# One encoder layer on one core: the rows of the input projection dealt to partitions in another order, each chunk loaded by eight DMAs

## The reference, cut to what matters

```
mod = silu(c) @ w_cond + b_cond                      # 6 x 1024: shift, scale, gate, twice
h   = LN(x) * (1 + scale_m) + shift_m
proj = h @ w_in                                      # w_in: 1024 x 8208
qa, ka, va, ga, lra, qb, kb, vb, gate_a, gate_b = split(proj)
log_a = log_sigmoid(lra @ w_gla_a2 + b_gla_a) / 16   # lra: columns 3072..3087 of w_in
mix = w_out( sig(gate_a) * w_branch_a(GLA) + sig(gate_b) * w_branch_b(StickBreak) )
x   = LN1(alpha * x + gate_m * mix)
x   = LN2(alpha * x + gate_f * HierMoE(h2))          # 32 experts, each 1024x512, 1024x512, 512x1024
```

## Time and profile before

| | |
|---|---|
| runs | 1111.52 us median of 3 (1110.47 to 1113.07) |
| the profiled execution | 1114.87 us, span 1113.1 us from first to last instruction |
| busy, share of the span | PE 83%, PEld 57%, DVE 32%, ACT 29%, POOL 31% |
| granted TensorE clock | mean 0.926 of full speed |
| `w_in` chunks | 16 DMAs of 2 MB, median 13.8 us from issue to landing |
| stages | head to about 43 us, `w_in` groups to about 428 us, branches and output to about 544 us, routing to about 600 us, experts to the end |

### The profile page before, as it was taken

How to read it: one execution, slowest core, us unless ns; L and a number is a source line. 1 busy time by engine, 2 the same in 40 slices (tenths; PEclk the granted TensorE clock), 3 DMA queues, 4 the chain that set the end, 5 groups by cost and what they waited for, 6 DMA issues and landing times.

```text
span 1113.1 us, 14515 instructions
## 1 busy us (share of the span) xinstructions
PE 927.2 (83%) x5835; PEld 639.0 (57%) x5843; DVE 355.6 (32%) x763; ACT 318.9 (29%) x496; POOL 343.7 (31%) x280
## 2 busy tenths in 40 slices
PE   3888999898998988998656999999988888888840
PEld 3677989895997987788643344343433333333310
DVE  4200155926322124453564222222211211122108
ACT  2372343351886587233131010000000000000001
POOL 7544467760342434457100111111111111111011
PEclk9898999998999999899856999999999999999985
DMA  9726525438476753257653999999999999999832
GB/s 332 231 76 115 111 78 111 96 98 235 144 156 231 170 209 115 85 178 290 248 223 113 395 424 425 426 425 426 424 425 426 425 428 426 424 426 426 364 144 61
DMA packets 60820, 294.10 MB, mean 264 GB/s; under 512 B 7541, under 2 KB 9165, under 8 KB 48162
## 3 DMA queue, kind: packets, MB, share of 16 engines
q1 hardware_dynamic: 49296, 272.68, 66.3%
q0 software_dynamic: 6560, 11.45, 3.0%
q10 hardware_dynamic: 4914, 9.28, 2.4%
HBM read 290.22 MB, written 14.68 MB: 274 GB/s over the span
## 4 chain that ended last, share of the span: by engine, by line
PE 49%; DMA 30%; DVE 9%; ACT 6%; issue 4%; SPq 1%; POOL 1%; ACTq 0%; POOLq 0%; DVEq 0%
DMA ring<-in_w_exp_up 20%; PE bank L1363 13%; PE bank L1028 7%; PE bank L1029 6%; PE bank L1030 6%; PE bank L1386 5%; DMA ring<-in_w_in 5%; DMA cond_slot<-in_w_cond 4%; PE bank L981 1%; PE bank L1353 1%; DVE hf L1878 1%; PE bank L1083 1%; DMA ring<-expert_rows 1%; PE bank L1375 1%; DVE stats L1440 1%
## 5 line engine op out<-in xcount | busy, mean ns | idle before, releaser
L517 POOL TENSOR_TENSOR w_lo<-ring,w_hi 128x1024 fp32r<-128x1024 f32 x88 | 210.7, 2407 | 214.8 <-ACT w_hi L727 214.5
L1363 PE MATMUL bank<-ring,hf 128*64 128x512 f32 x1024 | 232.5, 607 | 23.0 <-DMA ring<-in_w_exp_up 22.0
L1028 PE MATMUL bank<-h_hi,w_hi 128*128 128x320 f32 x576 | 188.3, 327 | 20.1 <-POOL w_lo L517 7.9
L1030 PE MATMUL bank<-h_hi,w_lo 128*128 128x320 f32 x576 | 182.5, 317 | 0.0
L1363 PEld LDWEIGHTS bank<-ring,hf 128*64 128x64 f32 x1024 | 82.0, 140 | 170.6 <-issue 169.4
L1386 PE MATMUL bank<-ring,he 128*64 128x512 f32 x512 | 127.5, 643 | 0.9 <-DVE he L1882 0.5
L1028 PEld LDWEIGHTS bank<-h_hi,w_hi 128*128 128x128 f32 x576 | 112.6, 195 | 25.6 <-ACT va L668 5.8
L1029 PE MATMUL bank<-h_lo,w_hi 128*128 128x320 f32 x384 | 122.1, 318 | 0.0
L566 POOL DMA_INDIRECT xrow<-expert_inputs,sidx x32 | 32.7, 1022 | 263.3 <-DVE sidx L1868 263.3
L1030 PEld LDWEIGHTS bank<-h_hi,w_lo 128*128 128x128 f32 x576 | 112.4, 195 | 0.0
L727 ACT ACTIVATE w_hi<-ring 128x1024 fp32r<-128x1024 f32 x88 | 92.6, 1054 | 46.5 <-DMA ring<-in_w_in 27.6
(11 more groups left out here) (366 smaller groups left out, 1264.3 us busy)
## 6 DMA issues: line engine op xcount, KB each, us to landing
ring<-in_w_exp_up SPq DMA_DIRECT2D x32, 2048.0 KB, 34.8
ring<-in_w_exp_down SPq DMA_DIRECT2D x32, 2048.0 KB, 34.1
ring<-in_w_exp_gate SPq DMA_DIRECT2D x32, 2048.0 KB, 30.2
ring<-in_w_in SPq DMA_DIRECT2D x16, 2048.0 KB, 13.8
cond_slot<-in_w_cond SPq DMA_DIRECT2D x9, 2048.0 KB, 11.0
ring<-in_w_cond SPq DMA_DIRECT2D x3, 2048.0 KB, 17.1
ring<-in_w_branch_b SPq DMA_DIRECT2D x2, 2048.0 KB, 7.8
ring<-in_w_branch_a SPq DMA_DIRECT2D x2, 2048.0 KB, 10.1
```

The lines of the kernel that those rows point to most:

```text
L517: pool.tensor_tensor(w_lo[slot][:, :, c], raw[:, :, c], w_hi[:, :, c].bitcast(F32), ALU.subtract)\
L1028: mm(b, hi[:, k, c], x_hi[:, k, :], start=(k == 0), stop=False)
L1030: last = mm(b, lo[:, k, c], x_hi[:, k, :], start=False, stop=(k == KT - 1))
L1363: last = mm(bank[1][64 * q:64 * q + 64, :], xg[:, k % 4, k // 4, :], ring[s + q][:, k * FF:k * FF + FF], start=(k == 0), stop=(k == KT - 1 ...
```

## The change

Within each k-tile the 128 features are dealt to the partitions in another order: with `128 k + 16 i + e` for a feature (`i` of 8, `e` of 16), it now lies on partition `8 e + i`. The chunks of `w_in` and the low-rank columns are loaded by eight DMAs each, one for every `i`: DMA `i` writes partitions `i`, `i + 8`, ..., `i + 120`, of each eight runs (one a k-tile), and reads sixteen neighbouring rows of every k-tile. The other matrices are loaded as before. To match, the normalised `x` is written in the dealt order (DVE), the shift and scale rows are copied into `crow` in the dealt order (ACT, chunks 0 to 3), and the sixteen bias rows of shift and scale are loaded once more, dealt by a DVE copy and turned by a TensorE transpose of their own, for which the first transpose's successor waits (`bias_ready`). The load of the low-rank columns moves from ACT's queue to SP's, behind the four `w_cond` chunks of the head and ahead of the first `w_in` chunk.

```diff
--- before.py
+++ after.py
@@ -54,6 +54,7 @@
 NORM_BANKS = ((3, 4), (1, 2), (3, 4))
 NORM_ORDER = (0, 1, 3, 2, 4, 5)
 COND_ORDER = (0, 2, 1, 3)
+IN_PARTS = 8
 
 
 EXTRA = ("cr", "ct", "vat", "vbt")
@@ -219,6 +220,8 @@
         lraT = ab[1][0:32, 0:T]
         wa2 = sp_[1][0:32, :]
         rows = ab[0][:, 0:P]
+        bias_rows = ab[0][0:16, P:2 * P]
+        bias_spread = ab[0][0:16, 2 * P:3 * P]
         xt = vb
         xn = on
         ck = wgt
@@ -304,7 +307,7 @@
         bank = [ctx.enter_context(nc.psum_tensor(f"bank{i}", [P, 512], F32)) for i in range(8)]
 
 
-        names = """const_ready rows_in x_in lra_in misc_in vecs_in x1_in cols_t silu_ready mod_ready xn_ready xn_t xt_ready
+        names = """const_ready rows_in bias_ready x_in lra_in misc_in vecs_in x1_in cols_t silu_ready mod_ready xn_ready xn_t xt_ready
             h_dve h_act h_pool hi_ready lo_ready lra_hi lra_lo h_moved ob_hi_ready ob_lo_ready cond_in
             proj_ready taken_act taken_dve xla_ps la_ready b_ps b_ready dec_ready exp_ready pd_ready lev_ps
             lev_taken lev_added kd_ready ke_ready ke_t ket_ready st_ps st_ready qe_ready go_ps go_ready ck_t
@@ -338,10 +341,18 @@
 
         USED = ("gu_ps", "gu_ps", "down_ps")
 
+        def loads(slot, upto):
+
+            return sum(IN_PARTS if c[0] == "in" else 1 for c in DENSE[:upto] if c[2] == slot)
+
+        def spread(block):
+
+            return block.rearrange("r (e i) -> r i e", i=IN_PARTS)
+
         def arrived(i):
 
             slot = DENSE[i][2]
-            return (S["cond_in"] if slot == COND_SLOT else chunk_in[slot]), 16 * sum(c[2] == slot for c in DENSE[:i + 1])
+            return (S["cond_in"] if slot == COND_SLOT else chunk_in[slot]), 16 * loads(slot, i + 1)
 
         def base(e):
 
@@ -349,7 +360,7 @@
 
         def expert_use(s, turn):
 
-            before = sum(c[2] == s for c in DENSE) if s <= HI_SLOT else 0
+            before = loads(s, ND) if s <= HI_SLOT else 0
             return 16 * (before + turn + 1)
 
         USES = [len(range(b, E, 3)) for b in range(3)]
@@ -376,7 +387,14 @@
             sp.dma_start(rows[0:8, :], a["c_prompt"].rearrange("a (k p) -> (a k) p", p=P)).then_inc(S["rows_in"], 16)
             sp.dma_start(rows[8:16, :], a["c_sample"].rearrange("a (k p) -> (a k) p", p=P)).then_inc(S["rows_in"], 16)
             sp.dma_start(rows[16:64, :], a["b_cond"].rearrange("a (k p) -> (a k) p", p=P)).then_inc(S["rows_in"], 16)
+            sp.dma_start(bias_rows, a["b_cond"].rearrange("a (k p) -> (a k) p", p=P)[0:16, :]).then_inc(S["rows_in"], 16)
             sp.dma_start(rows[64:72, :], a["gla_norm_g"].rearrange("a h (j p) -> (a h j) p", p=P)).then_inc(S["rows_in"], 16)
+
+            def rows_apart(dst, c0, c1, signal):
+
+                src = SRC["in"].rearrange("(k i e) n -> i e k n", k=KT, i=IN_PARTS)
+                for i in range(IN_PARTS):
+                    sp.dma_start(dst[i::IN_PARTS], src[i][:, :, c0:c1]).then_inc(signal, 16)
 
             def freed(i):
 
@@ -387,6 +405,8 @@
 
             for i in sorted(range(ND), key=freed):
                 name, c0, slot = DENSE[i]
+                if i == 4:
+                    rows_apart(w_lra[:, :, :], 3072, 3088, S["lra_in"])
                 before = [n for n in range(i) if DENSE[n][2] == slot]
                 if before:
                     sp.wait_ge(*consumed(before[-1]))
@@ -394,8 +414,11 @@
                     sp.wait_ge(S["go_ps"], 6)
                     sp.wait_ge(S["st_ready"], 4)
                 src = SRC[name].rearrange("(k p) n -> p k n", p=P)[:, :, c0:c0 + CB]
-                dst = cond_slot if slot == COND_SLOT else ring[slot]
-                sp.dma_start(dst[:, :].rearrange("p (k n) -> p k n", k=KT), src).then_inc(arrived(i)[0], 16)
+                dst = (cond_slot if slot == COND_SLOT else ring[slot])[:, :].rearrange("p (k n) -> p k n", k=KT)
+                if name == "in":
+                    rows_apart(dst, c0, c0 + CB, arrived(i)[0])
+                else:
+                    sp.dma_start(dst, src).then_inc(arrived(i)[0], 16)
 
 
             sp.wait_ge(S["proj_ready"], group_index("bb", KT - 1) + 1)
@@ -631,7 +654,6 @@
             act.dma_start(xt[:, 0:2, :], a["x_prompt"][0].rearrange("(t p) d -> p t d", p=P)).then_inc(S["x_in"], 16)
             act.dma_start(xt[0:64, 2, :], a["x_sample"][0]).then_inc(S["x_in"], 16)
             act.wait_ge(S["const_ready"], 1)
-            act.dma_start(w_lra[:, :, :], a["w_in"][0].rearrange("(k p) n -> p k n", p=P)[:, :, 3072:3088]).then_inc(S["lra_in"], 16)
             act.dma_start(wa2[0:RANK, :], a["w_gla_a2"][0]).then_inc(S["lra_in"], 16)
             act.dma_start(wa2[RANK:RANK + 1, :], a["b_gla_a"]).then_inc(S["lra_in"], 16)
             act.wait_ge(S["cols_t"], 1)
@@ -646,7 +668,10 @@
                 src = bank[n % PROJ_BANKS]
                 act.wait_ge(S["proj_ready"], n + 1)
                 if name == "cr":
-                    ins = X.activation(crow[:, :], src[:, 0:P], ACT.Copy)
+                    if i < 4:
+                        ins = X.activation(spread(crow[:, :]), src[:, 0:P].rearrange("r (i e) -> r i e", i=IN_PARTS), ACT.Copy)
+                    else:
+                        ins = X.activation(crow[:, :], src[:, 0:P], ACT.Copy)
                 elif name == "ct":
                     ins = X.activation(mod[:, 4 * i:4 * i + 4, :], src[:, 0:P].rearrange("p (m c) -> p m c", c=32)[:, :, 0:2],
                                        ACT.Copy)
@@ -693,7 +718,7 @@
                     take("ct", c)
 
             take_cond(COND_ORDER[0:2])
-            act.wait_ge(S["lra_in"], 48)
+            act.wait_ge(S["lra_in"], 16 * IN_PARTS + 32)
             X.activation(w_lra_hi[:, :, :], w_lra[:, :, :], ACT.Copy).then_inc(S["lra_hi"], 1)
 
             def modulate(k):
@@ -955,8 +980,10 @@
 
 
             pe.wait_ge(S["const_ready"], 1)
-            pe.wait_ge(S["rows_in"], 64)
-            nc.tensor.transpose(bank[7][:, 0:72], rows[0:72, :], ident[0:72, 0:72]).then_inc(S["cols_t"], 1)
+            pe.wait_ge(S["rows_in"], 80)
+            nc.tensor.transpose(bank[7][:, 0:72], rows[0:72, :], ident[0:72, 0:72])
+            pe.wait_ge(S["bias_ready"], 1)
+            nc.tensor.transpose(bank[7][:, 72:88], bias_spread, ident[0:16, 0:16]).then_inc(S["cols_t"], 1)
 
             g = [0]
 
@@ -1459,18 +1486,23 @@
                 ch.add(V.scalar_tensor_tensor(out=r, in0=q, scalar=1.5, in1=r, op0=ALU.add, op1=ALU.mult))
                 ch.done()
 
+            dve.wait_ge(S["rows_in"], 80)
+            V.tensor_copy(spread(bias_spread), bias_rows.rearrange("r (i e) -> r i e", i=IN_PARTS)).then_inc(S["bias_ready"], 1)
             dve.wait_ge(S["const_ready"], 1)
             dve.wait_ge(S["x_in"], 32)
             for t in range(3):
                 last = tile_stats(t, xt[0:TR[t], t, :], TR[t])
             last.then_inc(S["nrm_sum"], 1)
             dve.wait_ge(S["silu_ready"], 1)
-            ch.add(V.tensor_copy(cols[:, :], bank[7][:, 0:72]))
+            for c in (slice(0, 16), slice(32, 72)):
+                ch.add(V.tensor_copy(cols[:, c], bank[7][:, c]))
+            ch.add(V.tensor_copy(cols[:, 16:32], bank[7][:, 72:88]))
             reciprocal(1, 0, 3)
             for t in range(3):
                 n = TR[t]
-                V.tensor_scalar(xn[0:n, t, :], xt[0:n, t, :], mv[0:n, t, 0:1], rstd[0:n, t:t + 1], ALU.subtract,
-                                ALU.mult).then_inc(S["xn_ready"], 1)
+                V.tensor_scalar(xn[0:n, t, :].rearrange("r (k e i) -> r k i e", k=KT, i=IN_PARTS),
+                                xt[0:n, t, :].rearrange("r (k i e) -> r k i e", k=KT, i=IN_PARTS),
+                                mv[0:n, t, 0:1], rstd[0:n, t:t + 1], ALU.subtract, ALU.mult).then_inc(S["xn_ready"], 1)
 
             def take_mod(first, n):
                 ch.done()
```

## The result

The changed kernel takes 1129.72 us (median of 4 runs, 1127.77 to 1134.28) against 1111.20 before (median of 4, one more than in the table above); the ratio is 1.015 (95% interval 1.0116 to 1.0184). Run once more beside the kernel before, it came out at 1.0098 (1.0063 to 1.0134). It is slower by 1.0 to 1.5%, where 1107 was forecast. Its profiled execution took 1129.96 us, span 1128.2, 15.1 more than before; TensorE's mean clock is 0.916 against 0.926.

The account below looks back on a forecast made before the run. Slow `w_in` loads that are waited for were taken to bound the kernel before the experts. Loads gain 9.4 us, the head loses 4.9, net 4.5 off 1111.5: 1107.0 us; own range 1102 to 1112, with (a) and (b) 1096 to 1119.

Parts of the forecast that it names:

- What bounds the kernel: Before the expert stage: slow `w_in` loads that are waited for, with 13 to 16 us of TensorE idle to gain.
- The head: Start of the kernel: ACT waits for the moved low-rank columns, so `modulate(5)` starts at 41.8, 4.9 us later.
- the term L: In the head: time at which the low-rank columns land, 33.6 us, between 32.5 and 36.
- The loads: `w_in` chunks by eight DMAs: 12.7 us each, even and odd alike; 9.4 us gained in all.
- the terms 2.5, 1.1, 0.8, 4.3 and 2.7: Gains in us at `w_in` loads issued at 83.06, 126.20, ahead of 229.60, at 319.47 (with `cond_slot`), and at 374.20.
- the loss at the even load: Even `w_in` load issued at 233.40: 2.2 us longer, 2.0 us lost.
- The `cond_slot` term: Load issued at 319.47 and the `cond_slot` load behind it: 17.6 us together instead of 21.9, 4.3 us gained.
- (b): Rival: loads stay as slow on average as now and the head's 4.9 us decide, 1116.4 us; chance 0.22.
- (c): Rival: eight small DMAs or the new addresses make loads longer, 16.5 us, about 1141 us in all; chance 0.09.
- Rival (a): Memory was the whole cause and neighbouring rows cure it: 7.8 us a load, 1098.5 us in all; chance 0.27.

Follow-up runs that it names:

- even columns: Kernel before, each odd `w_in` chunk loaded from the columns 512 further left, so half the weights are those of other columns: 1092.69 us, ratio 0.9782.
- the run with one DMA: Changed kernel with one DMA a chunk in place of eight, low-rank columns still behind `w_cond` as one DMA: 1116.47 us, ratio 1.0029.
- the k-tile kernel: Kernel before, each `w_in` chunk loaded by eight DMAs, one a k-tile on all 128 partitions: 1110.57 us, ratio 0.9971; once more 1111.51 us, 0.9969.
- halves: Kernel before, each `w_in` chunk loaded in two halves of 256 columns, each issued when TensorE is done with its two groups: 1098.12 us, ratio 0.9856.

## Why the prediction was wrong

*What bounds the kernel* was right in kind: slow `w_in` loads, slow by their columns, waited for at the odd chunks. "There are some 13 to 16 us of TensorE idle to be had, and no more" was too low: even columns gave about 24. Gaps of TensorE alone do not count what the lower clock behind a gap costs (the stage behind the gap of 5.53 became 7.1 us shorter without it).

*The head* was right in its mechanism and too small. It was forecast at 4.9 us, with 3.8 to 7.3 as bounds, and measured 6.8. The landing of the low-rank columns, the term L, was put at 33.6 and came at 35.05; with four DMAs it was 31.64, with one 31.07. Whether the eight low-rank DMAs themselves or the first `w_in` DMAs behind them made it late was not separated, and no run shows the 1.5 us for eight semaphore updates that stood in its upper bound. The lower bound of 32.5 was wrong too, since it was taken from one profile: in the run with one DMA the fourth `w_cond` chunk had landed by 30.7. Two parts were too small in the sum: ACT's copy with a stride, put at nothing (0.38 us, 0.28 before), and TensorE's product, 3.35 us at a granted clock of 0.56 where 2.83, at 0.66, had been taken.

*The loads: the step that failed.* The limit of a DMA that reaches part of the partitions was right for even loads: 12.7 us forecast, 12.4 to 13.5 measured, and the runs with 16 neighbouring partitions, with 32 at a stride of four and with other rows show that this is the cause. In its size there was luck: the earlier trace rows had shown half the rate, in stores, for half the partitions, and each new DMA writes an eighth of them; the forecast doubled the data part without a row that says why two and not eight. The run with 16 neighbouring partitions shows that their number does not give the rate. By the Trainium skill ("SBUF — State Buffer", section on the DMA port swizzle) the three patterns reach four, eight and sixteen ports, and the rates of 121, 206 to 214 and 282 GB/s agree with that order. That rule is what carries the factor of two, and the prediction had it only beside the sum. What failed is "I take this ... for even and odd alike". The odd loads have a limit of their own in their columns, 176 GB/s, which lies below that of the partitions; a new limit of 214 cannot lift them. A load runs at the lower of its limits, and I had put one in the place of the other. So the terms 2.5, 1.1, 0.8, 4.3 and 2.7 of the sum, 11.4 us, lost their cause, and of them only 2.5 us at the `cond_slot` load came: the stage from 319.47 to 348.36 became one from 338.18 to 364.61. Of this 1.3 us are shorter gaps, and 1.3 the product behind them, 1.95 us for 3.22, at the full clock. The gaps of the terms 2.5, 1.1 and 0.8 grew instead, by 0.5, 0.5 and 1.7, and the stage from 374.20 stayed 21.0 us long. Only the loss at the even load was real, and larger (the gap of 3.23 and a stage 4.6 us longer, 2.0 forecast). In place of 9.4 us gained, the loads lost 1.6 on balance, besides the 6.7 of the clock.

*The `cond_slot` term* (4.3) failed for a second reason. Only the next chunks were said to wait behind the eight issues on SP; the `cond_slot` loads do too, and an issue took 0.60 us and the last ones of an odd load 1.0 to 2.0, not 0.4.

*What was not in the forecast at all* are the low-clock stretches, 3.5 and 3.2 us in the first profile. In all six profiles of kernels with eight or four DMAs that reach part of the partitions the stretch after the third odd chunk is at 0.87 or below; in all five with one DMA a chunk (the kernel before among them) it is at 1.00; of the two profiles of the k-tile kernel, which are of the very same code, one has it at 1.00 and the other at 0.87. So the stretch goes with the partial DMAs often, but not with them alone, and chance has a part in it. The second one has no such tie: the changed kernel has it in one of its two profiles, and the run with even columns, one DMA a chunk, has 27.0 us at 0.87 from 180.81 on. What sets either off is not settled: the idle gap before the first was 7.97 (neighbouring partitions), 2.55 and 2.73 (the changed kernel twice), 2.69, 2.21, 1.96 and 1.69 us in profiles that had it, and 2.05, 1.97, 2.22, 2.15 and 1.66 in profiles that had not; the 27.0 us of the even columns had no gap of TensorE over 1.5 us before them.

*The rivals.* The result lies beyond (b), the head's loss alone at 1116.4, and is in kind a mild (c), loads longer than now, the even ones above all. Rival (a), neighbouring rows as a cure, is refuted: rows 8 apart load as fast as neighbours. The row pitch rule of the Trainium skill ("DMA: Bandwidth & Descriptors"), that I had put beside (a), is measured there on pitches of 512 KiB and more, while the rows of `w_in` lie 32,832 bytes apart (8208 columns of four bytes); the runs do not test the rule, only what I had made of it. And they are against that: in six microseconds of the third to fifth odd load the rate was 171 to 175 GB/s in the changed kernel, 175 to 177 with rows 8 apart, 174 to 178 by k-tile, 178 to 182 with four DMAs and 174 to 178 before; only sixteen neighbouring partitions are slower, and for all chunks. Why columns at an odd multiple of 512, and the second half of them most, are slow stays open; no run changed the pitch or the start of the matrix.

## What to carry to other kernels

A load has several limits at once (the addresses it reads, the partitions it writes, the order on its queue). Before dealing it out anew, find for each kind of load which is the lowest, and forecast with the lowest that is left, not with the one that the change touches. Eight DMAs in place of one did no harm here as long as each reached all 128 partitions (261 GB/s, 255 with one); on sixteen of them it matters which, 214 GB/s at a stride of eight and 121 side by side. Where a double buffer is late, handing it back in halves can give much of what a faster load would (15 of some 24 us here) without touching the load, and a small load that is wanted early should not be put behind large ones on their queue: that alone cost 3 us.

## What the runs showed that was not expected

- DMAs behind a load on the same queue can delay it: the fourth `w_cond` chunk was there at 33.4 to 34.8 us in the three kernels that have eight `w_in` DMAs of 16 partitions right behind it, and at 31.2 to 32.5 with one DMA, halves or k-tiles behind it.
- An issue of a DMA on 16 partitions at a stride of eight took 0.60 us, of a k-tile on all 128 partitions 0.43, of a whole chunk 0.37. In the odd loads, which move slowly, the last two or three of eight issues took 1.0 to 2.0 us in both kinds, and what stands behind them on SP waits.
- `w_in` columns that start 512 further right load at 176 instead of 255 GB/s, whatever the slot, and this costs about 2.2% of the kernel (1.5 to 2.9%); the last 256 of each 1024 are the slowest, 85 to 91 GB/s by themselves.
- Sixteen neighbouring partitions: 121 GB/s; sixteen at a stride of eight: 206 to 214; 32 at a stride of four: 282.
